# Seven products instead of eight for pairs of feed-forward tiles: a single-core two-block transformer kernel

## The reference, cut to what matters

```
h = rms_norm(x, norm_ffn_pre_g[l])                       # stage 1, first block
f = (jax.nn.silu(h @ w_gate[l]) * (h @ w_up[l])) @ w_down[l]
x = x + rms_norm(f, norm_ffn_post_g[l])

x = x + 0.5 * swiglu(rmsnorm(x, ffn1_norm[l]), ...)       # stage 2, second block
x = x + 0.5 * swiglu(rmsnorm(x, ffn2_norm[l]), ...)       # stage 3, second block
```

## Time and profile before

| | before |
|---|---|
| device time, median of 3 | 1945.75 us |
| profiled execution | 1944.65 us, span 1942.9 us |
| PE busy | 1922.1 us (99%) |
| weight loads busy (PEld) | 1564.8 us (81%) |
| DVE / ACT / POOL busy | 52% / 39% / 12% |
| TensorE's granted clock | 0.998 |

### The profile page before, as it was taken

The page is one execution under the profiler, slowest core; times in us unless marked ns, Lnnn a source line. Parts: engine busy times, 40 slices in busy tenths (PEclk is TensorE's granted clock), DMA queues, the critical chain, the costliest instruction groups (busy, mean ns, idle before and its releaser), DMA issues.

```text
span 1942.9 us, 23941 instructions
## 1 busy us (share of the span) xinstructions
PE 1922.1 (99%) x9634; PEld 1564.8 (81%) x9634; DVE 1003.3 (52%) x1503; ACT 757.4 (39%) x1171; POOL 241.0 (12%) x242
## 2 busy tenths in 40 slices
PE   9999999999999999999999999999999999999998
PEld 7777788878888888788888888777787788888887
DVE  6677535373334345733333366887754454334335
ACT  6344533453223233432322356665543343233224
POOL 6210001201011011010110112222010011011010
PEclk9999999999999999999999999999999999999999
DMA  6122233433333323333333232222232233333323
GB/s 175 57 66 66 62 96 103 119 98 98 98 97 98 98 85 111 92 96 96 97 98 98 81 110 70 66 66 66 87 98 64 77 96 95 96 95 96 97 60 104
DMA packets 340767, 176.32 MB, mean 91 GB/s; under 512 B 6481, under 2 KB 339378, under 8 KB 340658
## 3 DMA queue, kind: packets, MB, share of 16 engines
q1 hardware_dynamic: 340658, 174.79, 30.8%
HBM read 172.67 MB, written 2.10 MB: 90 GB/s over the span
## 4 chain that ended last, share of the span: by engine, by line
PE 92%; DVE 4%; ACT 2%; issue 1%; DMA 1%; POOL 0%; SPq 0%; ACTq 0%; DVEq 0%
PE ps L1122 28%; PE ps L1126 28%; PE ps L1124 28%; PE ps L1189 1%; PE ps L1169 1%; PE ps L1178 1%; PE ps L1274 1%; PE ps L1135 1%; PE ps L1292 1%; DVE WL L1589 1%; PE ps L1203 1%; PE ps L1159 0%; DVE TS L1640 0%; PE ps L1152 0%; DVE L L1690 0%
## 5 line engine op out<-in xcount | busy, mean ns | idle before, releaser
L1122 PE MATMUL ps<-HH,WH 128*128 128x512 f32 x1728 | 686.2, 397 | 0.5 <-ACT HH L1345 0.4
L1126 PE MATMUL ps<-HL,WH 128*128 128x512 f32 x1728 | 674.7, 390 | 0.9 <-DVE HL L1610 0.8
L1124 PE MATMUL ps<-HH,WL 128*128 128x512 f32 x1728 | 674.1, 390 | 0.7 <-DVE WL L1589 0.7
L1589 DVE TENSOR_TENSOR WL<-RAW,WH 128x1024 fp32r<-128x1024 f32 (+3 forms) x335 | 400.3, 1197 | 530.1 <-ACT WH L1335 529.7
L1335 ACT ACTIVATE WH<-RAW 128x1024 fp32r<-128x1024 f32 (+3 forms) x335 | 337.6, 1010 | 518.4 <-PE ps L1126 514.5
L1122 PEld LDWEIGHTS ps<-HH,WH 128*128 128x128 f32 x1728 | 324.6, 188 | 75.8 <-issue 8.7
L1126 PEld LDWEIGHTS ps<-HL,WH 128*128 128x128 f32 x1728 | 324.5, 188 | 71.5 <-DVE HL L1610 2.1
L1124 PEld LDWEIGHTS ps<-HH,WL 128*128 128x128 f32 x1728 | 324.7, 188 | 70.5 <-issue 4.1
L1122 PE MATMUL ps<-GH,WH 128*128 128x512 f32 x688 | 269.6, 392 | 0.0
L1126 PE MATMUL ps<-GL,WH 128*128 128x512 f32 x688 | 268.4, 390 | 0.0
L1124 PE MATMUL ps<-GH,WL 128*128 128x512 f32 x688 | 268.2, 390 | 0.0
(11 more groups left out here) (214 smaller groups left out, 1535.4 us busy)
## 6 DMA issues: line engine op xcount, KB each, us to landing
RAW<-in_ffn_w_gu SPq DMA_DIRECT2D x88, 512.0 KB, 3.8
RAW<-in_w_in SPq DMA_DIRECT2D x67, 512.0 KB, 3.7
RAW<-in_ffn_w_down SPq DMA_DIRECT2D x32, 512.0 KB, 3.9
RAW<-in_w_gate SPq DMA_DIRECT2D x22, 512.0 KB, 3.8
RAW<-in_w_up SPq DMA_DIRECT2D x22, 512.0 KB, 3.8
RAW<-in_w_out SPq DMA_DIRECT2D x16, 512.0 KB, 4.2
RAW<-in_mem_w_kv SPq DMA_DIRECT2D x16, 512.0 KB, 3.9
RAW<-in_w_down SPq DMA_DIRECT2D x16, 512.0 KB, 4.1
```

The source lines that it names most:

```text
L1122: e.matmul(bk, wh, xh, start=k == 0, stop=False)
L1124: e.matmul(bk, wl, xh, start=False, stop=False)
L1126: last = e.matmul(bk, wh, xl, start=False, stop=k == kt - 1)
L1589: e.tensor_tensor(at.weight(n, "L"), m["RAW"][:, n % NRAW, 0:kt, :], at.weight(n, "H").bitcast(F32), ALU.subtract).then_inc(*sg.inc("lo", n))
```

## The change

**Pairs.** In each stage 6 pairs of neighbouring tiles (f, f+1) are treated together: tiles 5,6 of the first third; 0,1, 3,4 and 6,7 of the second; 0,1 and 3,4 of the third. A pair has a gate slot and an up slot, 12 slots in a stage, 36 in the kernel. A slot was 2 items of 24 matmuls with 512 columns. It becomes 7 products of 4 chunks by 3 matmuls, with 256 columns each: 84 matmuls. The two raw weights of a slot and the operand are cut into a 2x2 scheme (tile, half of the contraction, half of the tokens), and 7 products of sums replace 8 plain ones.

**What feeds them.** POOL makes four sums of weights for a slot (`combine_weights`, 128x512 each), in tiles of the ring. ACT and DVE split 7 half items (128x512) instead of 2 whole ones (128x1024). The ring WH/WL keeps its size, now counted as 6 halves. A weight sum may be ordered up to 8 items ahead.

**What follows them.** DVE adds the products up in five steps of 256 columns (`sum_one` one, `sum_two` two, `sum_three`, `sum_four` one each), ACT copies bank a once (`sum_one`). Product 5 is accumulated in bank a and waits for that copy, product 6 in bank c and waits for `sum_two`. For the gate slot Silu runs in three pieces on ACT; for the up slot POOL multiplies two pieces (`gate_mixed`) and DVE one (`corner`).

**The operand.** The first 5 tiles of a stage are plain, as before. Beside them DVE computes N = x times gain times R (`normal`, 8 chunks), POOL mixes it (`mix`, four subtractions of 256 columns per chunk pair), and ACT and DVE split the mixes into NH and NL (`mix_split`): one chunk pair each after tiles 0, 1, 2 and 3. During the up product of tile 4, ACT and DVE replace HH and HL by the split of N, chunk by chunk (`place`). Later plain tiles need no R and no `gate_r`.

**Memory.** NH and NL lie over L, PT, AT, masks, Dm and reset; `consts` 3 to 10 move behind the last third of stage 2 (`LATE`).

The core of the diff:

```diff
+MIX_AT = ((0,), (1,), (2,), (3,), ())
+PLAIN = len(MIX_AT)
+PAIRS = ((5,), (0, 3, 6), (0, 3))
+LOOK = 8
+MIXED = (("b", 2), ("c", 0), ("a", "11"), ("e", 1), ("d", 3), ("a", "21"), ("c", "22"))
...
+    def weigh_pair(self, key, name, c0):
+        n, r = len(self.weights), len(self.raws)
+        self.raws += [(name, 0, KD, c0 + P), (name, 0, KD, c0)]
+        self.weights += [("sum", key, 2), ("sum", key, 1), ("half", r + 1, 0), ("sum", key, 3), ("half", r, 1), ("half", r + 1, 1),
+                         ("sum", key, 4)]
...
     def split_to(self, n):
         while self.n_split < min(self.total, n):
-            while self.n_dma < min(self.total, self.n_split + NRAW):
+            i, known = self.n_split, self.known
+            while self.n_dma <= known.needs[i] or self.n_dma < min(len(known.raws), known.spent[i - 1] + NRAW if i else NRAW):
                 self.dma()
...
+            while self.n_dma < min(len(known.raws), known.spent[i] + NRAW):
                 self.dma()
+            whole = 0
+            for w, need in zip(known.weights[i + 1:i + 1 + LOOK], known.needs[i + 1:i + 1 + LOOK]):
+                whole += w[0] not in ("sum", "half")
+                if w[0] == "sum" and need < self.n_dma and whole < 2:
+                    self.combine_to(w[1], max(w[2], self.combined.get(w[1], 0)))
+
+    def ahead(self, n):
+        i = self.n_split
+        while i < self.total and self.known.offsets[i + 1] - HALVES_OF_RING <= self.known.offsets[n]:
+            i += 1
+        self.split_to(i)
...
+    def pair(self, gen, G, f, up, name, c0, pending):
...
+        self.ahead(n)
+        for i, (b, op) in enumerate(MIXED):
...
+            self.step("product", gen, key, i, n + i)
+            if i < 2 and pending:
+                self.split_tile(*pending.pop(0))
+            elif i == 2:
+                self.step("sum_one", key, n)
+            elif i == 3:
+                self.step("sum_two", key, n)
+            elif i == 4:
+                self.step("sum_three", key, n)
+                ...  # up: gate_mixed 1; gate: silu_mixed 1
+            elif i == 5:
+                self.step("corner", key, n)
+            elif i == 6:
+                self.step("sum_four", key, n)
+                ...  # up: gate_mixed 0; gate: silu_mixed 0
+            self.ahead(n + i + 1)
...
                 self.step("gate_r", key, go, R)
-                if not n == f == 0:
-                    mu, = self.mtiles([su], ("H", gen, 0), [bu])
-                self.step("gate_up", key, mu, bu)
+                if f:
+                    self.mix_split(gen, f - 1)
...
+                if f:
+                    mu, = self.mtiles([su], ("H", gen, 0), [bu], ahead=f < PLAIN - 1)
+                if f == PLAIN - 1:
+                    self.place(gen)
+                    self.ahead(len(self.weights))
+                self.step("gate_up", key, mu, bu, ("gr", key))
                 self.banks.give(bu, ("gu", key))
                 self.split_tile(("gt", key), ("gu", key), "G", G, f)
                 self.tiles.give(("gt", key), ("xl", ("G", G, f)))
+                if f < PLAIN - 1:
+                    self.mix(gen, f, gcol)
...
+    def product(gen, key, i, n):
...
+            e.matmul(bk, wh[:, c, :], xh, start=i < 5 and c == 0, stop=False, skip_group_check=i >= 5)
+            e.matmul(bk, wl[:, c, :], xh, start=False, stop=False, skip_group_check=i >= 5)
+            o = e.matmul(bk, wh[:, c, :], xl, start=False, stop=c == 3, skip_group_check=i >= 5)
...
+    def combine_weights(key, j):
...
+        g.wait_ge(*sg.at(f"d_raw{rb % NRAW}", rb))
+        g.wait_ge(*sg.at(f"d_raw{ra % NRAW}", ra))
...
+        e.tensor_tensor(out, x, y, op).then_inc(*sg.inc("comb", (key, j)))
```

More of the change, by code:

```diff
@@ L160, in mtiles @@
         if ahead:
-            self.split_to(n + cnt + NSPL)
+            self.ahead(n + cnt)
         return [("mm", n + i) for i in range(cnt)]
@@ L381, in pipeline, with normal, mix @@
             step()
-    def ffn(self, gen, gate, g0, up, u0, down, evac, third0):
-        R = None
+    def normal(self, gen, c, gcol):
+        self.tiles.take(("N", gen, c))
+        self.step("normal", gen, c, gcol + c, self.norm(gen))
+    def mix(self, gen, f, gcol):
+        for c in MIX_AT[f]:
+            self.normal(gen, c, gcol)
+            self.normal(gen, c + 4, gcol)
+            for a in range(2):
+                self.tiles.take(("mix", gen, c, a))
+            self.step("mix", gen, c)
@@ new lines, in mix_split, with place @@
+    def mix_split(self, gen, f):
+        for c in MIX_AT[f]:
+            for a in range(2):
+                self.step("mix_split", gen, c, a, self.mixed_free)
+                self.tiles.give(("mix", gen, c, a), ("op_lo", (gen, c, a)))
+    def place(self, gen):
+        n = len(self.weights) - 1
+        self.by_chunk.add(n)
+        for c in range(KD):
+            self.step("place", gen, c, ("mm", ("k", n, c) if c < KD - 1 else n))
+            self.tiles.give(("N", gen, c), ("xl", ("H", ("n", gen), c)), ("mixed", (gen, c % 4, 3)))
@@ L387, in ffn @@
+    def ffn(self, gen, gate, g0, up, u0, down, evac, third0, gcol):
+        R, pending = None, []
         for n, (f0, nf) in enumerate(THIRDS):
@@ L425, in ffn @@
                 evac(n, mt, b, mm)
-                self.split_to(len(self.weights) + NSPL)
+                if n == 2 and gen == 2:
+                    for i in LATE[mt]:
+                        self.step("consts", i, done)
+                self.ahead(len(self.weights))
             self.gfree = (mm,)
@@ L602, in gate @@
             return gates[br, mt]
-        consts = iter(range(9))
+        consts = iter(range(2))
         def more_consts():
@@ new lines, in split, with mix_split, place @@
+        e.activation(at.weight(n, "H"), at.raw(n), ACT.Copy).then_inc(*sg.inc("hi", n))
+    def mix_split(gen, c, a, free):
+        g.wait_ge(*sg.at("mixed", (gen, c, 2 + a)))
+        wait_all(free)
+        e.activation(m["NH"][:, 2 * a:2 * a + 2, c, :], blocks(at.tile(("mix", gen, c, a)), 256), ACT.Copy).then_inc(*sg.inc("op_hi", (gen, c, a)))
+    def place(gen, c, free):
+        g.wait_ge(*sg.at("N", (gen, c)))
+        g.wait_ge(*sg.at(*free))
+        e.activation(m["HH"][:, c, :], at.tile(("N", gen, c)), ACT.Copy).then_inc(*sg.inc("xh", ("H", ("n", gen), c)))
@@ L1592, in split_half, with sum_four @@
+    def sum_four(key, n):
+        G_, f, up = key
+        u = at.tile(("u", key))
+        out = u if up else at.tile(("gt", (G_, f)))
+        g.wait_ge(*sg.at("mm", n + 6))
+        if not up:
+            wait_all(at.tile_free(("gt", (G_, f))))
+        e.tensor_tensor(out[:, 256:512], at.bank(("pr", key, "c"))[:, 0:256], u[:, 256:512], ALU.add).then_inc(*sg.inc("part_sum", ("c12", key)))
     def split_half(a):
```

377 lines of the change are left out of this document (312 added, 65 removed).

## The result

The kernel with pairs takes **1968.35 us** (median of 4 runs, 1967.48 to 1969.17), the one before, beside it on the same chip, 1946.07. The ratio is 1.0113 [1.0096, 1.0131]: 22 us slower, where 11 us faster was forecast, and 20 us above the end of the range.

What follows compares the result with a forecast made beforehand. PE, busy 99% of the span, was taken as the bound. From the profiled 1944.65 us, -28.8 + 16.5 + 1 gave 1933.4, or 1934.5 us for the median of runs; range 1926 to 1941, chance 0.50.

Steps and rivals of the forecast that it cites:

- term 1: All 36 slots: 84 matmuls at 0.120 us replace 48 of 512 columns, 10.88 to 10.08 us a slot, gaining 28.8 us.
- Rival D: Products' 256-column distance does not hold: at 0.130 us nothing is gained, 1962 us; chance 0.14 together with Rival B.
- Waits inside slots: Products 5 and 6 and up slots' splits: PE waits of 1 us in all, bounds 0 and 9 us.
- term 2: Way into each stage's first pair: PE late some 5.5 us a stage, 16.5 in all; bounds 2 and 24.
- The mechanism that was named: Before the first pair: two up-slot weight sums on POOL ahead of tile 3's `gate_r`, which ends at 11 instead of 5.1.
- Edits at nothing: `mix` and `normal` of tiles 0 to 2, loads, moved masks and tile ring: counted as costing nothing.
- its sum for a pair: Two slots: mutually exclusive time of DVE, 9.6 us, and POOL, 10.9 us, together 20.5 of 20.2 us.
- Rival B: Each pair: exclusion of DVE and POOL costs 1.0 us a slot, 1959 us; chance 0.14 together with Rival D.
- A: Rival, first pairs: everything hides and PE does not wait, 1919 us, or 1917 with nothing; chance 0.22.
- C: Rival, pair slots: about half of Rival B's cost, 0.3 us a slot, with term 2: 1944 us, no change; chance 0.14.
- The masks: Behind stage 2: 13 us of moved POOL work recovers beside down items; otherwise the next norm waits up to 3 us.
- The signs named for a wrong forecast: No PE idle in first pairs, idle in products 5 and 6 of later pairs, or matmul distance above 0.125 us.

Runs made afterwards that it cites:

- e16: Kernel with pairs, with only POOL's weight sums replaced by write-only memsets (the mixes stay real): 1944.82 us.
- e10: Kernel with pairs, with only the up slot's weight sums held back until `place` is planned: 1964.5 us.
- e8: As e7, and the up slot's weight sums are also held back until `place` is planned: 1960.69 us.
- e7: Kernel with pairs, with `normal` and `mix` of a tile moved right behind its `gate_r`, before the up product: 1960.17 us.
- e2: Kernel with pairs, with no weight sums ordered ahead while a stage's five plain tiles are planned: 1980.16 us.
- e5: Kernel with pairs, without any pair slots or weight sums but with all preparation of the operand: 1968.34 us.
- e14: Kernel with pairs, with no pair in the first third (30 slots), mixes after tiles 0 to 3, `place` in tile 6, tile 7 plain: 1925.71 us.
- e18: As e11, but with more, smaller memsets to lengthen POOL's work (16 of 32 columns a sum, 8 a mixing step): 1934.48 us.
- e11: Kernel with pairs, POOL's weight sums and mixing steps replaced by write-only memsets, its two waits inside a mix left out: 1932.22 us.
- e12: The write-only replacement of e11 made in e8's order (mix early, up sums held): 1926.01 us.
- e17: Kernel with pairs, with only the mixing steps replaced by memsets, waits inside a mix gone, weight sums real: 1950.35 us.
- e4: Kernel with pairs, plus 60 unread matmuls on PE before product 0 of each stage's first pair: 1968.79 us.

## Why the prediction was wrong, step by step

- **The products** (term 1). Right: starts lie 0.120 us apart in every pair wherever PE doesn't wait and the clock is full, 461.42 to 461.54 to 461.65 above, and an undisturbed slot takes 10.08 us. Rival D is out.
- **Waits inside slots.** 1 us forecast, 2.8 measured, inside its bounds of 0 and 9. They lie in four of the 15 later pairs and go away in e16. Product 5 waits for the copy in first pairs only, 1.6 us each.
- **The way into the first pair** (term 2). This is the step that failed: 5.5 us a stage forecast, 16 measured, 16.5 against 47.9 in the sum. Its upper bound of 8 was too low by half. In the first pair of stage 1, product 0 waits 8.2 us (1.8 forecast), and everything behind it stretches as well. The mechanism that was named is there, sums ahead of `gate_r` and `gate_up` waiting (4.66 us on ACT), but holding it off brought little: with those sums held back product 0 waits 2.7 us a stage less, and 1.3 us a stage of it arrive (e10), or nothing once the mix is early (e8 against e7). Its price by itself was not measured, since both runs only move the sums. The first wrong figure of the chain is DVE's split of up item 4, forecast to end 2.44 us after gate item 3 and measured at 8.9: DVE stood in the preparation of tile 2. (A small slip besides: two `normal` of 0.75 us from 13.1 end at 14.6, not 14.4.)
- What stood in its place was two omissions. The first: the working put 0 at the end of gate item 3 and took all engines as on time there. **"Edits at nothing"** let `mix` and `normal` of tiles 0 to 2 hide in DVE's free half. They don't use up DVE's time but lie on a circle of 10.7 us per 10.88 us tile (e2, e5, e14), the late start of the stage was never made up, and it was 5.0 us late at tile 2. Preparation alone costs 22 us (e5). The second: exclusion was read correctly from the earlier trace rows and its sum for a pair was made, but on the way into the pair it was charged with a single 0.6 us. There POOL is busy 37 of 59 us, and the two-input DVE instructions take some 10 us longer than undisturbed ones of their shape. Windows of 423 to 482 us, the kernel after:

```profile
423.00:482.00 59.00, 48.92 (x231) 41.40 (x229) 44.06 (x49) 23.37 (x38) 36.51 (x29) 0.91 0.18 52
```

and e18:

```profile
423.00:482.00 59.00, 54.72 (x298) 47.19 (x297) 43.47 (x63) 28.87 (x51) 22.23 (x261) 1.00 0.26 74
```

  DVE's busy time is the same 44 us, but in after it does 49 instructions in it and in e18 63. Removing the reading (and some length, and two waits in each mix) gives back 34 to 36 us (e18, e11), the better order behind that another 6 (e12).
- **Rival B** had the cause and the wrong place. It charged each pair with the exclusion (1959). But 11 of the 15 later pairs run at full speed and four lose 2.8 us in all, where B had 36; that the plain tile between them pays, as the prediction argued, fits this and was not tried alone. The first pair has four mixes and 16 splits just ahead of it. B's sum took 2 us a stage for term 2, not the forecast's 5.5; with 5.5 it would have been 1969.5 us, next to the measured time and by luck alone. **A** and **C** fell with term 2.
- **The masks** and the later loads cost nothing that shows: spans differ by 23.0, and pairs account for 21.9.
- The signs named for a wrong forecast looked at products 5 and 6 of later pairs and at none before product 0 of the first. The view that would have shown it is a budget of the stretch *ahead* of the first consumer, per engine, with exclusive time of DVE and POOL added up, and the length of the round trip.

Left open: the order on POOL is worth 8 us (e7), write-only POOL 36 (e11), both 42 (e12); first pairs still take 23.3 us then, 3.1 over 20.16. But no run takes the circle away, they only shorten it (10.4 us in e7, 9.4 in e11), so how much of the 36 us went through the circle and how much through DVE's own queue was not separated; e17, with the circle at 9.4 us and the sums reading, gives 18. The share of POOL's length is an estimate, and the waits inside a mix were not removed alone. The half clock costs 2 to 3 us a stage where PE has work in store (e5), and about 0.2 us in the one first pair where it was absent (e4, stage 3).

## What to carry to other kernels

Before a saving is counted, follow the preparation's round trip through all engines: if it is about as long as the period it hides in, a late start is never made up, however idle each engine looks, and the first consumer needs distance more than a better order (e14 gave up a sixth of the saving and kept nearly all of the rest). Where GpSimd reads SBUF beside VectorE instructions with two SBUF inputs, add their times as if they were one engine's, for the busiest stretch and not for the average. When a change has a set-up and a steady part, time each alone: the set-up without the saving (e5) tells in one run whether the idea can pay.

## What was unexpected of the hardware

- POOL instructions that only write do not hold DVE off: its split stays at 703 ns (e18) where reading ones make it 931. The Trainium skill (SBUF — State Buffer, "SBUF: two separate sides") states this limit: a VectorE instruction with two SBUF inputs takes the shared port "only against a GpSimd op that reads SBUF". The runs agree. The prediction used the rule for its exclusion but not as a way to test it.
- Short POOL writes cost more than their share: 512 columns take 0.52 us as one memset, 0.74 as 8 of 64 columns (e11) and 1.00 as 16 of 32 (e18; one each 0.063 us).
- Behind a wait of 8.2 us the granted clock was 0.50 (1.2 GHz) for the first 6.3 us of matmuls, and 256 columns took 0.213 us instead of 0.120. In e4 it was 0.50 from 473.78 on, behind waits of 1.09 and 1.06 us. Where PE has work in store behind the wait (e5, stage 1), 14 matmuls of 512 columns at half clock add 2.8 us to a wait of 4.5.
- With 256 columns a matmul with its weight load costs 0.120 us at full clock, 53% of one with 512; the weight loads (PEld busy 20.10 of 20.10 us in a pair) keep up.
